# A hybrid mixer block: the order of the recurrent strands, and where SSD's squares are summed

## The reference

```python
u = rms_norm(x, mix_norm[l]) @ w_in[l]
y = jnp.concatenate([y_ssd, y_ml, y_rw], axis=-1)
x = x + y @ w_out[l]
```

```python
y = y.reshape(bsz, t, SSD_WIDTH) * jax.nn.silu(z.astype(jnp.float32))
return group_rms_norm(y, norm_g, G).astype(u.dtype)
```

## Time and profile before

| | before |
|---|---|
| median of three runs | 1808.74 us (1806.51 to 1809.49) |
| the profiled execution: device time | 1808.37 us |
| its span | 1806.5 us |
| busy share PE, PEld, DVE, ACT, POOL | 96%, 90%, 69%, 49%, 20% |
| chain that ended last: PE, DVE, ACT | 83%, 11%, 3% |
| mean granted clock of TensorE | 0.979 |
| mixers of the two layers | about 250 to 495 us and 970 to 1215 us |

### The profile page before, as it was taken

How to read it: one execution, slowest core, us unless ns; L and a number is a source line. 1 busy time by engine, 2 the same in 40 slices (tenths; PEclk the granted TensorE clock), 3 DMA queues, 4 the chain that set the end, 5 groups by cost and what they waited for, 6 DMA issues and landing times.

```text
span 1806.5 us, 35596 instructions
## 1 busy us (share of the span) xinstructions
PE 1736.2 (96%) x15296; PEld 1621.6 (90%) x15296; DVE 1252.2 (69%) x2101; ACT 889.3 (49%) x1566; POOL 358.7 (20%) x308
## 2 busy tenths in 40 slices
PE   7999999999899999999999999989999999989997
PEld 6999988887799998999998888789999888879987
DVE  5876665866567776687676676656777665779974
ACT  5564435323345654566443533334655545556652
POOL 3552000000112651156200000011265200121110
PEclk9999999999799999999999999979999999989999
DMA  8655522211147565565562221014555542335442
GB/s 302 237 218 193 212 94 94 89 33 46 48 160 256 210 238 185 207 258 202 196 228 73 99 90 48 25 48 165 223 225 214 195 180 105 117 132 183 175 154 104
DMA packets 44492, 282.86 MB, mean 157 GB/s; under 512 B 6064, under 2 KB 6704, under 8 KB 17712
## 3 DMA queue, kind: packets, MB, share of 16 engines
q1 hardware_dynamic: 44336, 280.60, 42.7%
HBM read 279.53 MB, written 1.05 MB: 155 GB/s over the span
## 4 chain that ended last, share of the span: by engine, by line
PE 83%; DVE 11%; ACT 3%; issue 1%; DMA 1%; POOL 0%; SPq 0%; DVEq 0%; ACTq 0%
PE bank L489 16%; PE bank L491 15%; PE bank L490 15%; PE bank L497 10%; PE bank L985 7%; PE bank L498 5%; PE bank L1581 4%; DVE WL L480 2%; ACT WH L475 2%; PE bank L527 1%; PE bank L1848 1%; PE bank L1125 1%; DVE XC L1054 1%; DMA ring<-wst 1%; PE bank L1858 1%
## 5 line engine op out<-in xcount | busy, mean ns | idle before, releaser
L489 PE MATMUL bank<-XNH,WH 128*128 128x256 f32 (+1 forms) x2176 | 621.7, 286 | 17.7 <-DVE XNL L573 12.2
L480 DVE TENSOR_TENSOR WL<-ring,WH 128x2048 fp32r<-128x2048 f32 (+1 forms) x235 | 508.6, 2167 | 166.8 <-ACT WH L475 166.5
L491 PE MATMUL bank<-XNH,WL 128*128 128x256 f32 (+1 forms) x2176 | 617.2, 284 | 0.0
L490 PE MATMUL bank<-XNL,WH 128*128 128x256 f32 (+1 forms) x2176 | 615.2, 283 | 0.0
L475 ACT ACTIVATE WH<-ring 128x2048 fp32r<-128x2048 f32 (+1 forms) x235 | 405.5, 1729 | 217.4 <-PE bank L491 152.7
L489 PEld LDWEIGHTS bank<-XNH,WH 128*128 128x128 f32 x2176 | 413.5, 190 | 23.7 <-DVE XNL L573 12.4
L490 PEld LDWEIGHTS bank<-XNL,WH 128*128 128x128 f32 x2176 | 415.1, 191 | 0.0
L491 PEld LDWEIGHTS bank<-XNH,WL 128*128 128x128 f32 x2176 | 414.8, 191 | 0.0
L497 PE MATMUL bank<-HP,WH 128*128 128x512 f32 x770 | 267.6, 392 | 0.8 <-POOL HP L882 0.7
L498 PE MATMUL bank<-HP,WL 128*128 128x256 f32 x770 | 215.4, 280 | 0.0
L985 PE MATMUL bank<-XN,ring 128*128 128x256 f32 x832 | 200.3, 389 | 0.0
(11 more groups left out here) (474 smaller groups left out, 2615.3 us busy)
## 6 DMA issues: line engine op xcount, KB each, us to landing
ring<-wst SPq DMA_DIRECT2D x206, 1024.0 KB, 4.8
ring<-wst SPq DMA_DIRECT2D x80, 704.0 KB, 4.1
LP<-lp SPq DMA_DIRECT2D x1, 1872.0 KB, 7.0
LP<-lp SPq DMA_DIRECT2D x1, 1792.0 KB, 8.6
X<-xin SPq DMA_DIRECT2D x2, 512.0 KB, 4.5
out<-X SPq DMA_DIRECT2D x4, 256.0 KB, 2.5
C<-cst SPq DMA_DIRECT2D x1, 193.0 KB, 10.6
AL<-cst SPq DMA_DIRECT2D x1, 192.0 KB, 10.6
```

Source lines behind the costliest of these rows:

```text
L480: e.do.tensor_tensor(WL[:, slot[q], 0:n], ring[:, i % NSLOT, 0:n], WH[:, slot[q], 0:n].bitcast(F32), ALU.subtract).then_inc(*w_dve.up("low ...
L489: e.do.matmul(o, WH[:, s, cols], xh, start=first, stop=False)
L490: e.do.matmul(o, WH[:, s, cols], xl, start=False, stop=False)
L491: return e.do.matmul(o, WL[:, s, cols], xh, start=False, stop=last)
```

## The change

Three edits. In the list of turns, the mLSTM turn `scan more` comes before the first of the two `ssd` turns of a round instead of behind it, and `proj end` (which serves `proj` from its 80th step on) stands at two more places. SSD's squares get two additions per group on GpSimd (128x512, then 128x256, in place), so that PE's sum takes 4 matmuls instead of 16. And SSD's strand gets idle steps so that the sum comes one step later, and all behind it two steps later.

```diff
-    turns = [..., "lane0", "proj more", "lane1", "ssd", "scan more", "lane2", "scan", "lane3", "ssd",
-             "proj end", "lane0 chunk", "lane1 chunk", "ssd end", "proj chunk", "lane2 chunk", "lane3 chunk", "ssd end", "fin", "ahead"]
+    turns = [..., "lane0", "proj more", "lane1", "scan more", "ssd", "proj end", "lane2", "scan", "lane3", "ssd",
+             "proj end", "lane0 chunk", "lane1 chunk", "ssd end", "proj chunk", "lane2 chunk", "lane3 chunk", "ssd end", "proj end", "fin", "ahead"]
...
+            for _ in range(3):
+                yield
             for g in range(2):
-                e.wait_ge(*d_act.on("sq", l, g))
+                e.wait_ge(*d_pool.on("squares", l, g))
                 for c in range(2):
-                    for i in range(4):
-                        s = T * i + c * 128
-                        m = e.do.matmul(b[:, 2 * g + c:2 * g + c + 1], (xd, xe)[g][:, s:s + 128], ones[:, 0:1], start=i == 0, stop=i == 3)
+                    m = e.do.matmul(b[:, 2 * g + c:2 * g + c + 1], (xd, xe)[g][:, 128 * c:128 * c + 128], ones[:, 0:1], start=True, stop=True)
...
         def pool_ssd(e, l):
-            for _ in range(32):
+            for _ in range(25):
+                yield
+            for g in range(2):
+                q = (xd, xe)[g]
+                e.wait_ge(*d_act.on("sq", l, g))
+                e.do.tensor_tensor(q[:, 0:512], q[:, 0:512], q[:, 512:1024], ALU.add).then_inc(*d_pool.up())
+                e.wait_ge(*d_pool.last())
+                e.do.tensor_tensor(q[:, 0:256], q[:, 0:256], q[:, 256:512], ALU.add).then_inc(*d_pool.up("squares", l, g))
+            for _ in range(9):
                 yield
```

More of the change, by code:

```diff
@@ L210, in order_of @@
     lanes = [f"lane{j}" for j in range(4)]
-    turns = ["proj", "rwkv", "rwkv more", "lane0", "proj more", "lane1", "ssd", "scan more", "lane2", "scan", "lane3", "ssd",
-             "proj end", "lane0 chunk", "lane1 chunk", "ssd end", "proj chunk", "lane2 chunk", "lane3 chunk", "ssd end", "fin", "ahead"]
+    turns = ["proj", "rwkv", "rwkv more", "lane0", "proj more", "lane1", "scan more", "ssd", "proj end", "lane2", "scan", "lane3", "ssd",
+             "proj end", "lane0 chunk", "lane1 chunk", "ssd end", "proj chunk", "lane2 chunk", "lane3 chunk", "ssd end", "proj end", "fin", "ahead"]
     def allowed(turn, done):
@@ L1864, in pe_ssd @@
                     yield
-            yield
-            yield
+            for _ in range(3):
+                yield
             for g in range(2):
-                e.wait_ge(*d_act.on("sq", l, g))
+                e.wait_ge(*d_pool.on("squares", l, g))
                 for c in range(2):
-                    for i in range(4):
-                        s = T * i + c * 128
-                        m = e.do.matmul(b[:, 2 * g + c:2 * g + c + 1], (xd, xe)[g][:, s:s + 128], ones[:, 0:1], start=i == 0, stop=i == 3)
+                    m = e.do.matmul(b[:, 2 * g + c:2 * g + c + 1], (xd, xe)[g][:, 128 * c:128 * c + 128], ones[:, 0:1], start=True, stop=True)
             m.then_inc(*d_pe.up("sums", l))
-            yield
-            yield
+            for _ in range(3):
+                yield
             e.wait_ge(*d_dve.on("rstd", l))
@@ L1913, in act_ssd @@
                 e.do.activation((xd, xe)[g].rearrange("p (n t) -> p n t", t=T), Y[:, 4 * g:4 * g + 4, :], ACT.Square).then_inc(*d_act.up("sq", l, g))
-            for _ in range(4):
+            for _ in range(6):
                 yield
@@ L1976, in dve_ssd @@
                 e.do.tensor_tensor(yo, yo, XC[:, 4 * g:4 * g + 4, :], ALU.mult).then_inc(*d_dve.up("gated", l, g))
-            yield
-            yield
+            for _ in range(4):
+                yield
             e.wait_ge(*d_pe.on("sums", l))
```

## The result

The changed kernel takes 1797.56 us, the median of 6 runs (1795.19 to 1798.70). The kernel before took 1806.68 us in 6 runs beside it. The ratio is 0.9951, with a 95% interval of 0.9941 to 0.9962: 8.8 us faster, where I had forecast 4 us and a time of 1804.5. A second measurement gave 1800.01 us and a ratio of 0.9967 (0.9954 to 0.9979), 5.9 us faster, which is just inside the range of 1800 to 1813. The profiled execution took 1798.5 us (span 1796.5), with a mean granted clock of 0.984 for 0.979. TensorE was busy 1725.7 us for 1736.2.

What follows compares the result with a forecast made beforehand. TensorE, 96% busy, was taken as the bound, time changing only where it waits or runs at low clock. Per layer 3.3 − 1.2 = 2.1 us gained, 4.2 in both, off 1808.37: 1804.2, forecast as 1804.5 us, range 1800 to 1813.

Steps and rivals of the forecast that it cites:

- the tail: From the squares on: later squares, GpSimd additions and a broadcast 0.7 us later; 1.2 us lost per layer, bounds 0.5 to 2.9.
- other swapped pairs: At the other swapped turns, later mix additions or mixes keep nobody waiting: no cost, under 1 us if one showed.
- of the first place, the wait: At SSD's mix, a 4.0 us wait before L1858 becomes one of 3.4 before L1848: 0.6 us gained per layer.
- first place, wait and clock: At SSD's mix, shorter wait plus 2.75 us from a shorter low clock: 3.3 us gained per layer, 0.6 to 5.0.
- rival (1): After the first wait the clock stays low as long as now: 1.2 us lost in all, 1809.9 us; chance 0.25.
- The price of the old stretch: At the first place, the old low clock covers some 8.8 us of TensorE work and costs 4.4 us per layer.
- the new price: At the first place, one low stretch of some 3.3 us, as in the third block, costs 1.65 us.
- (2): The clock doesn't fall at all after the first wait: 3.8 us gained per layer, 1801.1 us; chance 0.12.
- the half step: Behind the tail's broadcast, TensorE has half an S step that it had done before: 0.5 us.
- Rival (3): Slower: the stall of lanes 2 and 3 keeps the tail's clock low 3.3 us more, 1813.3 us; chance 0.15.
- Rival (4): The sums' saving counts in full, some 3 us per layer, as the lanes aren't held up: 1796 us; chance 0.06.
- The sums: In the tail, four matmuls for sixteen save 24 of 32 records, 3.6 us of TensorE, of which nothing is left.

Runs made afterwards that it cites:

- the swap alone: Only `scan more` moved ahead of the first `ssd`, no added `proj end`, old squares, against the kernel before: 1799.6 us, ratio 0.9963.
- all turns: The whole new list of turns with the old squares (16 matmuls, no GpSimd additions), against the kernel before: 1806.4 us, ratio 0.9998.
- before again: The kernel before once more, with no edit, for a second profile: 1805.1 us, ratio 0.9998.
- after again: The changed kernel once more, with no edit, for a second profile: 1800.0 us, ratio 0.9967 to the kernel before.
- the late split: The changed kernel with the first step of the strand that splits `w_out` allowed two SSD steps later: 1797.2 us, ratio 0.9945 to the kernel before.
- the late gate: The changed kernel with mLSTM's gate one step later on VectorE, behind SSD's mix addition: 1793.1 us, ratio 0.9933 to the kernel before.

## Why the prediction was wrong

The direction was right, the size was off by more than its range: 1797.6 where 1800 was the lower end. The step that failed is the tail, of which the sum said that it loses 1.2 us in each layer. Per layer, from the profiles of the table:

| term | predicted | measured |
|---|---|---|
| other swapped pairs | 0 | 0.4 gained |
| of the first place, the wait | 0.6 gained | 0.85 gained |
| first place, wait and clock | 3.3 gained | 2.7 gained |
| tail | 1.2 lost | 0.2 gained (0.4 in the first two profiles, 0.0 in the second two) |
| sum | 2.1 gained | 3.3 gained |

**The first place** went in kind as told: 3.4 us predicted before L1848 and 3.17 measured, no long wait before L1858, the first low stretch 3.4 us in place of 10.2. What the sum did not hold is the second stretch 3.4 us later, just behind the one-column sums, which 10 of 14 mixers have; rival (1) had named these sums. The price of the old stretch was too low as well. TensorE is busy in all of 452.8 to 463.1, not in 8.8 us of it, so by the same reckoning it cost 5.1 us and not 4.4. The stretch of the earlier trace rows that I took for the new price began at 1521.2, not 1521.6, and so lasted 3.4 us. So the gain is 2.7 us (24.88 as the mean of the six mixers with the old order, 22.13 of the 14 with the new one) rather than 3.3. Rivals (1) and (2) are both out. No run kept the wait and moved L985 alone, so that the early L985 is what ends the low stretch isn't shown; behind the same wait and with the same order it lasted 6.8 us once with the swap alone and once with all turns.

**The other pairs** brought 0.4 us that I had put at nothing: from L1737 of layer 0 to SSD's mix of layer 1 it takes 669.2 us in both profiles of before, and 668.8 in after and in the kernel with the swap alone.

**The tail is the step that failed.** Up to the broadcast its parts were right: the wait of lanes 2 and 3 (5.6 predicted, 5.69), the additions (4.4, and 4.7 from 472.00 to 476.71), the broadcast 0.7 us later, counted from mLSTM's second L527 (15.46 for 14.63 us, so 0.83). What failed is the sentence "Behind the broadcast TensorE has one half of an S step (0.5 us) that it had done before" and the 1.2 us lost that it leads to. From the broadcast to L1737 it takes not 0.5 us more but 1.1 less (10.39 in before, 9.25 in after; 10.61 and 9.37 in layer 1). The sum held the low clock of the tail fixed behind the broadcast. In before it was low for 4.7 us of that time, until 487.0; in after for 1.95 us, until 482.15. 2.8 us less at half speed is 1.4 us, most of the 1.6 that I missed. The other profiles bear this out. In the six mixers of before, before again and the swap the low clock covers 3.6 to 5.8 us of this time, and the time less half of the cover is 7.98 to 8.08 us each time; in the four of after and after again it covers 1.6 to 2.7 us, and the rest is 8.00 to 8.29 us. So the half step cost at most 0.3 us, and the clock gave back the rest. In after the fall comes within the long standstill, 6.8 to 7.9 us behind mLSTM's second L527, where it came at 7.4 to 9.6 in those six. Rival (3) named this wait and gave it the wrong sign: the low stretch did not become longer (10.2 us in both) but earlier. How early it comes varies: in the second profiles the two tails are equal (24.7 and 24.6 us before, 24.8 and 24.6 after).

**Rival (4)**, 1796 us, is nearest to the measured time, but by luck. Its condition, that the copies don't hold up the lanes, is refuted by the wait of 5.69 us.

**The sums.** I priced them at 4.79 us and called the saving lost. That is true with the split late (a tail of 22.0 us with the 16 matmuls, 23.9 with the additions) and without the two "proj end" (25.05 and 24.8). But behind the long wait that the new turns make, the same 32 records take 6.99 us, and there the short sums give back the 2.8 us per layer that the turns cost (27.5 to 24.7). The parts of the change can only be judged together. "The split of `w_out` now lies on that way" is shown by the late split.

**The base.** The sum stood against one profiled execution and the median of three runs, 1808.74 us; that of six was 1806.68, so 2.1 us of the miss are the base. In that profile the part behind the mixers, 593.9 us, was at the upper end of what later profiles show. Two layers at 3.3 us are 6.6 us; the two measurements of after gave 8.8 and 5.9. That the 3.0 us behind the mixers in the first pair come from the clock and not from the work is shown by the other profiles (590.8 to 593.9 for the same work); whether a kernel's timing favours one end of that isn't. Why the clock fell at 1463 in one kernel and not at 1456 in the other, and what decides on the second stretch at the first place, stays open.

## What to carry to other kernels

Where TensorE waits for some microseconds, ask where the low clock that follows will lie. Over an idle engine or a wait it costs nothing, over work of TensorE it costs half of its own length; so a shorter wait can gain twice (the late gate: 1.6 us of wait and as much of clock), and a longer one be nearly free. Before a one-column reduction is moved to another engine, see how much of its price is its own (3.6 us here at full clock, by my estimate) and how much is the clock's: it took 4.1 to 6.6 us behind waits of 1.7 us and 7.0 behind those of 3.9. Take the wait away first: here the condition on one turn was worth at least as much as the additions (ratios of 0.9940 for 0.9951 and 0.9967, tails of 22.0 for 24.7 us). And take more than one profile before a low stretch of it enters a sum.

## What the runs showed of the hardware

- The low clock lasted 6.8, 10.2 or 13.7 us after the wait of 4.0 us, and 3.4 or 6.8 after that of 3.2 us. It differs in one kernel too: 13.7 and 6.8 us in layer 1 of before. Over 29 timed runs beside the experiments, before took 1803.05 to 1809.77 us, with a mean granted clock of 0.982 in the first of these and 0.979 in the second.
- In the waits of 3.1 to 3.2 us (14 mixers) and 4.0 us (6), or within 1.5 us behind them, the clock fell in 19 of 20 cases; in the second mixer of the swap alone it fell 5 us later. With a wait of 1.6 us (8 mixers) it did not fall there; 5 of them had one stretch of 3.4 us later, behind the one-column sums, and 3 had none.
- VectorE and GpSimd held each other up for whole instructions. L1368 takes 0.75 us for two with GpSimd idle and 2.36 beside L1999. L2001 takes 0.73 and, begun within L480, 2.65. The Trainium skill's rule (SBUF — State Buffer, section Who interferes with whom) fits both. By that rule the prediction had let the first addition wait for both L1368. It did not: L1999 began at 472.00 and L1368 at 472.42, so the later one was VectorE's. The price that I had put on it, 0.7 us on GpSimd's side, fell mostly on VectorE's, where nobody waited for it.
